# Half of the router's turns and squares moved beside the output product before it

## The reference

```
h = h + mixed @ w_out                                # (528, 1024), the output product
hs = rms_norm(h, ffn_norm_g)
aff = softmax(hs @ w_router)                         # (528, 16)
g, idx = top_k(aff.T, 66)                            # each of 16 experts takes 66 tokens
xg = hs[idx]
y = (silu(xg @ w_gate) * (xg @ w_up)) @ w_down       # 16 experts, 402 MB of weights
h = h + scatter_add(g * y)
```

## Time and profile before

| what | value |
|---|---|
| median of 3 runs | 2184.02 us (2183.22 to 2184.87) |
| the profiled execution | 2185.32 us |
| its span | 2183.2 us |
| busy: PE, DVE, ACT, POOL | 99%, 76%, 64%, 16% |
| mean granted TensorE clock | 0.999 |
| output product, last part, to the stage's end | up to 266.05 us of the span |
| router's stage | 266.05 to 300.7 us |
| experts' stage and what follows | from 300.7 us |

### The profile page before, as it was taken

One profiled execution on the slowest core, in us unless ns is written; L12 is line 12 of the kernel. 1 busy time (PEld: TensorE's weight loads), 2 busy tenths in 40 slices (PEclk: granted clock), 3 DMA queues, 4 the chain that ended last, 5 costly groups with the idle time before them and its releaser, 6 DMA issues. The chain is left out here.

```text
span 2183.2 us, 31916 instructions
## 1 busy us (share of the span) xinstructions
PE 2157.2 (99%) x11509; PEld 1557.7 (71%) x11509; DVE 1653.6 (76%) x2155; ACT 1392.3 (64%) x1796; POOL 340.0 (16%) x209
## 2 busy tenths in 40 slices
PE   9999999999999999999999999999999999999999
PEld 9988765565565555655556555687897788888777
DVE  6456678998989989899898998756755556875664
ACT  5345577777777777767777777755555555676653
POOL 3032041211122111121111200330000000211000
PEclk9999999999999999999999999999999999999999
DMA  6213479999999999999999999522321131241301
GB/s 188 83 57 117 168 272 370 377 382 371 384 383 372 382 370 382 385 376 380 371 383 383 374 381 368 217 86 88 90 66 59 59 118 51 61 138 39 116 1 39
DMA packets 179672, 506.88 MB, mean 232 GB/s; under 512 B 12557, under 2 KB 57389, under 8 KB 179581
## 3 DMA queue, kind: packets, MB, share of 16 engines
q1 hardware_dynamic: 174829, 494.92, 60.8%
q0 software_dynamic: 4752, 10.75, 2.2%
HBM read 492.99 MB, written 10.48 MB: 231 GB/s over the span
## 5 line engine op out<-in xcount | busy, mean ns | idle before, releaser
L2252 DVE TENSOR_TENSOR pieces_low<-pieces,pieces_high 128x2048 fp32r<-128x2048 f32 x383 | 873.3, 2290 | 109.2 <-ACT pieces_high L2197 105.1
L2197 ACT ACTIVATE pieces_high<-pieces 128x2048 fp32r<-128x2048 f32 x382 | 729.1, 1917 | 237.8 <-PE ps L2121 231.2
L2121 PE MATMUL ps<-pieces_high,ex_x 128*66 128x512 f32 x2080 | 574.9, 393 | 1.1 <-PEq L1593 0.5
L2121 PEld LDWEIGHTS ps<-pieces_high,ex_x 128*66 128x66 f32 x2080 | 279.4, 136 | 195.6 <-issue 7.2
L2121 PE MATMUL ps<-pieces_low,ex_x 128*66 128x512 f32 x1040 | 323.6, 392 | 0.0
L2121 PE MATMUL ps<-pieces_high,ex_h 128*66 128x512 f32 x992 | 277.0, 393 | 0.0
L495 DVE TENSOR_TENSOR in_w<-ring,in_w 128x256 fp32r<-128x256 f32 (+2 forms) x276 | 125.1, 460 | 155.0 <-ACT in_w L482 153.1
L2593 PE MATMUL ps<-hn_split,in_w 128*128 128x512 f32 x864 | 221.3, 406 | 2.7 <-DVE in_w L495 1.6
L2121 PEld LDWEIGHTS ps<-pieces_low,ex_x 128*66 128x66 f32 x1040 | 141.6, 136 | 97.4
L482 ACT ACTIVATE in_w<-ring 128x256 fp32r<-128x256 f32 (+2 forms) x276 | 117.0, 426 | 127.2 <-PE ps L2593 57.2
L2121 PEld LDWEIGHTS ps<-pieces_high,ex_h 128*66 128x66 f32 x992 | 133.6, 136 | 90.4 <-DVE pieces_low L2252 3.2
(11 more groups left out here) (510 smaller groups left out, 2777.7 us busy)
## 6 DMA issues: line engine op xcount, KB each, us to landing
pieces<-in_w_gate SPq DMA_DIRECT2D x128, 1024.0 KB, 7.3
pieces<-in_w_up SPq DMA_DIRECT2D x128, 1024.0 KB, 7.7
pieces<-in_w_down SPq DMA_DIRECT2D x128, 1024.0 KB, 8.6
ring<-in_a_w_in SPq DMA_DIRECT2D x24, 1024.0 KB, 5.2
ring<-in_b_w_in SPq DMA_DIRECT2D x4, 2048.0 KB, 7.8
ring<-in_w_in SPq DMA_DIRECT2D x7, 1024.0 KB, 4.9
ring<-in_b_w_out SPq DMA_DIRECT2D x2, 3072.0 KB, 14.3
ring<-in_w_in SPq DMA_DIRECT2D x8, 512.0 KB, 3.6
```

The lines of the kernel that those rows point to most:

```text
L2121: ins = pe.matmul(ps[0:CAP, banks + c, :], parts[a][:, k0 + k, :], w[b][:, k, c * 512:(c + 1) * 512], start=start and k == 0 and a == b == ...
L2197: nc.scalar.activation(m.high[:, n % NSPLIT, :], m.pieces[:, n % NPIECE, :], ACT.Copy).then_inc(high_done, 1)
L2252: nc.vector.tensor_tensor(m.low_part[:, n % NSPLIT, :], m.pieces[:, n % NPIECE, :], m.high[:, n % NSPLIT, :].bitcast(F32), ALU.subtract).t ...
```

## The change

Of each tile the first half of the columns (complete after job 0) is turned and squared in the first stage. On TensorE `turn_first(0)`, `(1)` and `(2)` stand behind steps 12, 13 and 14 of the output product and turn tiles 0, 1 and 4 (the tail of 16 tokens); `turn_first(3)` and `(4)`, tiles 2 and 3, stand behind step 15, the last. They use banks 2, 3, 7, 3 and 2. ScalarE squares the halves (512 columns) at steps 12, 13 and 14 of its own order and takes the first three turned halves behind step 15; the other two it takes first thing in the router's stage. The sums go to `half_ss`, cleared by VectorE.

In the router's stage only the second halves are turned, evicted by VectorE (five copies instead of ten) and squared (512 columns instead of 1024). A new addition on VectorE, behind the last `take_parts`, joins the two sums ahead of the root. Step 0 of the memory product no longer stands inside the loop: all steps are behind the last logits, and `turn_scores` stands behind step 3 instead of 2. On ScalarE one high part more stands between the squares, one stands between the root and the exponential instead of four, and two follow the exponential.

```diff
+HALF_SLOT = (0, 2, 1, 3, 5)
+HALF_TURNS = ((0, 2), (1, 3), (len(TILES1) - 1, 7), (2, 3), (3, 2))
+def turn_half(m, pe, h, i):
+    t, bank = HALF_TURNS[i]
+    n = TILES1[t][1]
+    for k in range(4):
+        ins = pe.transpose(m.ps[:, bank, k * P:k * P + n], h[0:n, t, k * P:(k + 1) * P], m.ident[0:n, 0:n])
+    ins.then_inc(m.half_turned, 1)
+def take_half(m, act, ht0, i):
+    t, bank = HALF_TURNS[i]
+    t0, n = TILES1[t]
+    act.wait_ge(m.half_turned, i + 1)
+    m.nc.scalar.activation(ht0[:, :, t0:t0 + n], m.ps[:, bank, :].rearrange("p (k c) -> p k c", k=4)[:, :, 0:n],
+                           ACT.Copy).then_inc(m.half_taken, 1)
...
+            def turn_first(i):
+                if i == 0:
+                    pe.wait_ge(out.out["dve"], 4)
+                if i == 2:
+                    pe.wait_ge(tail_taken, 1)
+                    pe.wait_ge(mem_low, KD)
+                if i >= 3:
+                    pe.wait_ge(m.half_taken, 2)
+                turn_half(m, pe, tok, i)
+            for i in range(3):
+                work.setdefault(12 + i, []).append(lambda i=i: turn_first(i))
+            work.setdefault(15, []).extend([lambda: turn_first(3), lambda: turn_first(4)])
             out.products(pe, work, start=3)
...
+            def square_first(tiles):
+                act.wait_ge(half_cleared, 1)
+                for t in tiles:
+                    n = TILES1[t][1]
+                    act.wait_ge(*((tail_taken, 1) if t == tail else (out.out["dve"], t + 1)))
+                    nc.scalar.activation(half_junk[0:n, :], tok[0:n, t, 0:512], ACT.Square, scale=D ** -0.5,
+                                         accum_out=m.half_ss[0:n, HALF_SLOT[t]:HALF_SLOT[t] + 1]).then_inc(half_squared, 1)
+                    act.wait_ge(half_squared, t + 1)
+            for i, tiles in enumerate(((0, 1), (2, 3), (4,))):
+                work.setdefault(12 + i, []).append(lambda tiles=tiles: square_first(tiles))
+            for i in range(3):
+                work.setdefault(15, []).append(lambda i=i: take_half(m, act, ht0, i))
...
+            work.setdefault(8, []).append(lambda: nc.vector.memset(m.half_ss, 0.5).then_inc(half_cleared, 1))
...
             def parts(t):
-                pe.wait_ge(s["evicted"], 2 * t + 2)
+                pe.wait_ge(s["evicted"], t + 1)
+                if t in (1, 2):
+                    pe.wait_ge(m.half_taken, 4)
+                if t == 3:
+                    pe.wait_ge(m.half_taken, 5)
...
                 if t == 0:
                     pe.wait_ge(s["tables"], 1)
+                    pe.wait_ge(m.half_taken, 5)
...
-                if t == nt - 1:
-                    g.products(pe, stop=1)
...
-            g.products(pe, {2: [turn_scores], n_steps - 6: [turn_picks], n_steps - 2: [turn_x]}, start=1)
+            g.products(pe, {3: [turn_scores], n_steps - 6: [turn_picks], n_steps - 2: [turn_x]})
...
+            for i in (3, 4):
+                take_half(m, act, ht[0], i)
             act.wait_ge(s["cleared"], 1)
             for t in range(nt):
                 square(t)
-                if t >= 2 and t < nt - 1:
-                    g.high_of(act, t - 2)
+                if 1 <= t < nt - 1:
+                    g.high_of(act, t - 1)
+            act.wait_ge(s["sums_added"], 1)
             nc.scalar.activation(ss[:, 1, :], ss[:, 0, :], ACT.Sqrt, bias=m.eps[:, 0:1]).then_inc(s["root"], 1)
-            for i in range(2, NS):
-                g.high_of(act, i)
+            g.high_of(act, 3)
             act.wait_ge(s["shifted"], 1)
             nc.scalar.activation(aff[:], aff[:], ACT.Exp).then_inc(s["exped"], 1)
+            for i in range(4, NS):
+                g.high_of(act, i)
...
+            dve.wait_ge(s["squared"], nt)
+            nc.vector.tensor_tensor(ss[:, 0, :], ss[:, 0, :], m.half_ss, ALU.add).then_inc(s["sums_added"], 1)
             step(nc.vector.memset(aff[:], 0.0))
             dve.wait_ge(s["root"], 1)
```

More of the change, by code:

```diff
@@ L137, in __init__ @@
         self.cols = self.keep("cols", [P, 2, P])
-        self.eps = self.keep("eps", [P, 1])
+        small = self.keep("eps", [P, 8])
+        self.eps, self.half_ss = small[:, 0:1], small[:, 2:8]
         self.lam = self.keep("lam", [P, 1])
@@ L806, in first_layer_stage @@
     tail_out = lambda c, g: ps[32 * g:32 * g + TILES1[tail][1], 4, c * P:(c + 1) * P]
-    out_on_tensor, out_on_scalar, out_on_vector = beside
+    mem_low, out_on_tensor, out_on_scalar, out_on_vector = beside
+    half_junk = m.area("half_junk", [P, 512], 81920)
+    half_cleared, half_squared = m.sem("half_cleared"), m.sem("half_squared")
     o_bank = lambda t: 5 + t % 3
@@ L1078, in _ @@
             nc.scalar.activation(ss[:, 1, :], ss[:, 0, :], ACT.Sqrt, bias=m.eps[:, 0:1]).then_inc(s["root"], 1)
-            out.split("act", act, out_on_scalar(act), start=2)
+            def square_first(tiles):
[6 more added lines that the diff above has]
+                    act.wait_ge(half_squared, t + 1)
+            work = out_on_scalar(act)
+            for i, tiles in enumerate(((0, 1), (2, 3), (4,))):
+                work.setdefault(12 + i, []).append(lambda tiles=tiles: square_first(tiles))
+            for i in range(3):
+                work.setdefault(15, []).append(lambda i=i: take_half(m, act, ht0, i))
+            out.split("act", act, work, start=2)
         @block.vector
@@ L1518, in on_vector @@
         return work
-    return load, on_tensor, on_scalar, on_vector
+    return load, low, on_tensor, on_scalar, on_vector
 def memory_keys(m, rows, keys, at):
@@ L1542, in router_stage @@
     SLOTS, SEG = 6, 2 * P
-    slot = (0, 2, 1, 3, 5)
+    slot = HALF_SLOT
     at = small
@@ L1569, in router_stage @@
     turned = lambda i: ps[0:CAP, 6, i * NE:(i + 1) * NE]
-    junk = m.at("router_junk", [P, D], m.gaps[0])
+    junk = m.at("router_junk", [P, 512], m.gaps[0])
     gained_w = m.area("router_w_gained", [P, KD, 32], 90624)
     PART = (7, 3)
-    names = ("w_gained cleared squared root inverse normed turned evicted parts parts_taken tables logits shifted exped "
+    names = ("w_gained cleared squared sums_added root inverse normed turned evicted parts parts_taken tables logits shifted exped "
              "weighed turned_scores mine_spread picked picks_turned first_rows picks_taken gather_sent")
@@ L1631, in turn @@
                 n = TILES1[t][1]
-                for half in range(2):
-                    u = 2 * t + half
-                    if u >= 3:
-                        pe.wait_ge(s["evicted"], u - 2)
-                    for k in range(4):
-                        f = 4 * half + k
-                        ins = pe.transpose(ps[:, 4 + u % 3, k * P:k * P + n], h[0:n, t, f * P:(f + 1) * P],
-                                           m.ident[0:n, 0:n])
-                    ins.then_inc(s["turned"], 1)
+                if t >= 3:
+                    pe.wait_ge(s["evicted"], t - 2)
+                for k in range(4):
+                    ins = pe.transpose(ps[:, 4 + t % 3, k * P:k * P + n], h[0:n, t, (4 + k) * P:(5 + k) * P],
+                                       m.ident[0:n, 0:n])
+                ins.then_inc(s["turned"], 1)
             def parts(t):
                 t0, n = TILES1[t]
-                pe.wait_ge(s["evicted"], 2 * t + 2)
+                pe.wait_ge(s["evicted"], t + 1)
[3 more added lines that the diff above has]
+                    pe.wait_ge(m.half_taken, 5)
                 if t == 0:
@@ L1652, in parts @@
                         k = 4 * half + q
-                        ins = pe.matmul(ps[32 * q:32 * q + 32, PART[t % 2], 0:n], gained_w[:, k, :], ht[:, k, t0:t0 + n],
+                        ins = pe.matmul(ps[32 * q:32 * q + 32, PART[t % 2], 0:n], gained_w[:, k, :], ht[half][:, q, t0:t0 + n],
                                         start=(half == 0), stop=(half == 1))
@@ L1752, in _, with evict @@
                                     ALU.mult).then_inc(s["w_gained"], 1)
-            def evict(u):
-                t, half = divmod(u, 2)
+            def evict(t):
                 t0, n = TILES1[t]
-                dve.wait_ge(s["turned"], u + 1)
-                bank = ps[:, 4 + u % 3, :].rearrange("p (k c) -> p k c", k=4)[:, :, 0:n]
-                nc.vector.tensor_copy(ht[:, 4 * half:4 * half + 4, t0:t0 + n], bank).then_inc(s["evicted"], 1)
+                dve.wait_ge(s["turned"], t + 1)
+                bank = ps[:, 4 + t % 3, :].rearrange("p (k c) -> p k c", k=4)[:, :, 0:n]
+                nc.vector.tensor_copy(ht[1][:, :, t0:t0 + n], bank).then_inc(s["evicted"], 1)
             def take_parts(t):
@@ L1766, in _ @@
             for t in range(nt):
-                evict(2 * t)
-                evict(2 * t + 1)
+                evict(t)
                 if t:
@@ L3840, in two_blocks @@
         mem_split = m.area("mem_split", [P, KD, 2, MEM], 92160, F32R)
+        ht = [m.area(f"h_turned{i}", [P, KD // 2, L1], at) for i, at in enumerate((64512, 40960))]
```

8 lines of the change are left out of this document (4 added, 4 removed).

## The result

The changed kernel took 2187.48 us, the median of 20 runs (2185.19 to 2190.38), and the kernel before 2184.74 us in 20 runs beside it (2183.22 to 2186.31): a ratio of 1.0015 with a 95% interval of 1.0009 to 1.0021. That is 2.74 us slower, where 1.3 were forecast. It lies inside 0.2% and just outside the range. Part of the distance to the forecast of 2185.3 is its base: it was built on the median of three runs of before, 2184.02, where 20 runs give 2184.74. The profiled execution has a span of 2185.7 us against 2183.2.

The account below looks back on a forecast made before the run. TensorE's written order bounds up to `turn_scores`, then the chain of the picks. +1.25 us for the stage's start, -0.02 to `turn_scores`, 0 behind, with rounding +1.3: 2184.02 + 1.3 = 2185.3 us, range 2183.0 to 2187.4.

Parts of the forecast that it names:

- The stage's start: Start of the router's stage: 1.25 us later, from 1.08 for three turns and 0.17 for TensorE leaving last.
- 0.36 us for a turn: First stage, TensorE: each of three turns among the gapless output matmuls costs 0.36 us, 1.08 in all.
- 0.17 us for leaving: End of first stage: with two turns behind step 15, TensorE leaves last, 0.17 us after VectorE.
- The loop: Router's loop without step 0: memory product starts 7.62 us behind the stage's start, where steps 1 and 2 started at 10.00.
- The first wait: Start of the router's loop: a wait of 0.5 us at the first eviction.
- `logits` at 0.23 us: Router's loop, TensorE: each tile's `logits` product takes 0.23 us, as read from the profile before.
- turn_scores at 13.20: Behind four steps of memory product, 5.58 us: `turn_scores` 13.20 us behind the stage's start, against 13.22 before.
- The scores are ready at 11.4 and wait 1.8 us: Ahead of `turn_scores`: weighed affinities ready 11.4 us behind the stage's start, then waiting 1.8 us for step 3.
- behind step 2 this would be a gain: Placing `turn_scores` behind step 2 would gain, since the scores wait 1.8 us for step 3; as written, none.
- Behind turn_scores: `turn_scores` to `turn_picks` still 12.12 us with TensorE idle 1.7, then 6.77 to `turn_x`; adds 0 to the sum.
- Rival 3: TensorE's clock falls behind the router's small products: 1.5 us lost, 3 if twice, 2186.8 to 2188.3; chance 0.08.
- Rivals 1, 2 and 4: Loop without waits, faster, 2183.2 (0.17); scores wait for VectorE, slower, 2186.1 (0.08); nothing moves, 2184.0 (0.10).

Follow-up runs that it names:

- e2: Kernel before plus three turns of first halves behind steps 12, 13 and 14, router's stage still turning everything; +0.6 ± 0.7 us against the kernel before.
- e3: Kernel before plus five turns of first halves, two of them behind step 15, router's stage still turning everything; +1.3 ± 0.8 us against the kernel before.
- e7: Changed kernel with step 0 of the memory product back in the loop and `turn_scores` behind step 2; +1.7 ± 0.7 us over the kernel before.
- filled kernels: Changed kernel with unused matmuls in TensorE's waits: ahead of `turn_picks`, in the loop, or both; 1.7, 2.3 and 2.5 us over the kernel before.
- e5: Changed kernel with six unused matmuls ahead of `turn_picks`; +1.7 ± 0.7 us over the kernel before.
- e4: Kernel before with only `turn_scores` moved from behind step 2 to behind step 3; +1.6 ± 0.8 us against the kernel before.
- e9: Changed kernel with ten unused matmuls, four in the loop's waits and six ahead of `turn_picks`; +2.5 ± 0.7 us over the kernel before.
- e14: Kernel before with `turn_scores` behind step 3 and six unused matmuls ahead of `turn_picks`; +1.1 ± 0.6 us against the kernel before.

## Why the prediction was wrong, point by point

- **The stage's start** was put at +1.25 us and came at +1.40. The step "0.36 us for a turn" was under-sized: 0.42 in e2. The 0.17 us for leaving was right (0.14, e3 less e2), as was the 0.2 us by which ScalarE's squares delay one split at no cost.
- **The loop** was put at 7.62 us to the memory product and took 8.10. The first wait (0.35), that for the tables and those of the last two tiles (0.41, 0.30) are there. The term that failed is `logits` at 0.23 us: 270.91 to 271.20 is 0.29, 275.03 to 275.35 0.32, and the four come to 1.26 us instead of 0.92. That is 0.34 of the 0.48; the rest is 0.02 to 0.05 at a time in the turns and copies. The weight loads show what changed. Timelines of them (PEld) for one of these products, before and changed:

```profile
271.21 0.30 PEld L1663 LDWEIGHTS ps<-router_pick,router_part 128*128 128x128 f32 x2
```
```profile
272.26 0.30 PEld L1720 LDWEIGHTS ps<-router_pick,router_part 128*128 128x128 f32 x2
```

  Before, the load starts 0.11 us ahead of its product (271.32); changed, it starts 0.01 us ahead of it (272.27), and 0.03 at most in all four. The kernel before has one such case too, at 272.71, of 0.33 us, so the higher price was in its trace. Why the load comes late was not tried; most likely its operand has only just been copied.
- **"turn_scores at 13.20"** was 13.70, all of it from the loop. **"The scores are ready at 11.4 and wait 1.8 us"** was wrong: they were ready at 12.7. I left the last product of the affinities at 0.27 us, though the two high parts that now follow the exponential give GpSimd work just there. It did not decide, since step 3 ended later still; but it makes "behind step 2 this would be a gain" worth 0.9 us less than it said.
- **Behind turn_scores** 12.12 and 6.77 us and an idle 1.7 us were right: 12.10, 6.69, 1.49.
- The chain's sum was +1.3 and came out as +1.8: right in kind, and short by those two terms. The range was also closed too early: its own terms, 2184.02 + 2.8 + 0.8, give 2187.6 for its upper end, not 2187.4. That 2187.48 lies between the two is chance, and doesn't repair the account.
- **The clock** was the miss that counts. Rival 3 had mechanism, direction and size of one fall (1.5 us; 1.6 measured at 276 us), with a chance of 0.08, argued from one stretch of before in which the clock had held. In that stretch step 0 stood among the small products, which in the changed kernel it doesn't; with it put back and the scores behind step 2 (e7) the clock held too, and its runs have 0.5 falls each. The change adds two places of waits; in traces of such kernels the clock fell at one in three of seven and at the other in two of six, and the runs of the changed kernel have 1.2 falls more than those of before, worth 1.8 us. I had it as a rival instead of as a term of the sum, where it stood at nothing. Rivals 1, 2 and 4 did not happen.
- Between 256 and 303 us the granted clock fell only in traces where step 0 or the picks had left waits open. The Trainium skill, TensorE: Matmul & The Clock Gate, "The HAM clock gate", says that too little activity throttles the clock; the falls there agree in direction. The fall near 1450 us in the trace of before came behind 20 products of four columns, with TensorE busy 4.00 of the 4.00 us ahead of it by the records, so a busy row alone doesn't tell that the clock will hold.
- What stays open: chain (1.8) and filled kernels (2.15 ± 0.4) agree, and the mean clocks account for the 3.5 of the unfilled ones. The falls seen at the two places, 3/7 of 1.6 and 2/6 of 1.0 us, give 1.0 us of that gap; the traces don't settle where the other falls lie, near 1450 us or there as well.

## What to carry to other kernels

Where TensorE is busy in the stage that gives work away and in the one that receives it, moving work is a draw; count instead the time that it waits, before and after. A step of independent product inside a chain of small dependent products pays twice: it covers their copies, and it keeps the clock. When a change takes such cover away, put a fall of the clock into the sum with the share of executions that may see it, and time it in many runs, because one trace shows it or does not. The mean granted clock of each run, read against a few traces, counts the falls and parts their cost from that of the longer chain.

## What the runs showed of the hardware

- The granted clock of TensorE fell to 0.50 for 3.4 us (0.73 on average over 6 us in e5) in e5 behind small products with 1.4 us of waits among them and no step of large matmuls, and in e4 behind 1.5 us of idle time followed by ten small products; in some executions of one program, not in others. A fall cost 1.6 us at the first place and 1.0 at the second, and 1.5 ± 0.2 us in the fit over 168 runs.
- With ten unused matmuls of 512 columns in those waits it stayed at 1.00 there in the trace (e9, which has falls near 12 and 1452 us all the same), and the runs scatter by 1.0 us; six of them ahead of `turn_picks` took the falls from 14 in 11 runs (e4) to two (e14).
- A 96 column `tensor_tensor` with both inputs in SBUF takes 0.26 us beside an idle GpSimd, and up to 1.33 us beside GpSimd's subtraction of 1.3 us, which reads SBUF too.
- Four 128x128 transposes between matmuls of 512 columns cost 0.42 us of a full TensorE.
